# Two-layer attention-and-convolution trunk: moved squares add, head load, output-weight splits and sums

## The reference

```python
h = _rmsnorm(x, mix_norm_gain[l])
p = jnp.einsum('bsd,df->bsf', h, w_in[l])
q, k, v, conv_value, conv_gate = split(p)
q = _rope(_rmsnorm(q, q_norm_gain[l]), cos, sin)
k = _rope(_rmsnorm(k, k_norm_gain[l]), cos, sin)
attn = _dilated_attention(q, k, v)
u = conv_value * sigmoid(conv_gate)
c = silu(_layernorm(_causal_dwconv(u, conv_dw_kernel[l], conv_dw_bias[l]),
                    conv_ln_gain[l], conv_ln_bias[l]))
x = x + concat(attn, c) @ w_out[l]
h = _rmsnorm(x, ffn_norm_gain[l])
up, gate = split(causal_dwconv3(h @ w_up[l]))
x = x + (silu(gate) * up) @ w_down[l]
```

## Time and profile before

| | |
|---|---|
| median of 3 runs | 2270.85 us (2265.39, 2270.85, 2270.91) |
| profiled execution | 2272.27 us |
| its span | 2270.4 us |
| mean granted TensorE clock | 0.997 |
| TensorE busy | 2234.1 us, 98% |
| VectorE busy | 1792.8 us, 79% |
| ScalarE busy | 953.2 us, 42% |
| GpSimd busy | 131.6 us, 6% |

### The profile page before, as it was taken

The page is one execution under the profiler, slowest core; times in us unless marked ns, Lnnn a source line. Parts: engine busy times, 40 slices in busy tenths (PEclk is TensorE's granted clock), DMA queues, the critical chain, the costliest instruction groups (busy, mean ns, idle before and its releaser), DMA issues.

```text
span 2270.4 us, 31620 instructions
## 1 busy us (share of the span) xinstructions
PE 2234.1 (98%) x11128; PEld 1852.0 (82%) x11128; DVE 1792.8 (79%) x2266; ACT 953.2 (42%) x1454; POOL 131.6 (6%) x62
## 2 busy tenths in 40 slices
PE   7999999999999999999999999999999999999999
PEld 6888788888888888888888877888878888888887
DVE  5898886688777777778849998856987777777786
ACT  5322686454333333333432236755533333333331
POOL 0122001110000000000002210021000000000000
PEclk9999999999999999999999999999999999999999
DMA  4333641201111111111212245401011111111112
GB/s 155 100 88 98 177 103 29 74 19 40 54 56 55 55 55 55 55 51 42 93 38 84 84 130 158 112 11 65 19 56 56 56 50 42 55 55 55 55 40 108
DMA packets 47980, 158.25 MB, mean 70 GB/s; under 512 B 7568, under 2 KB 10256, under 8 KB 47888
## 3 DMA queue, kind: packets, MB, share of 16 engines
q1 hardware_dynamic: 47024, 154.64, 21.7%
q10 hardware_dynamic: 864, 2.36, 0.3%
HBM read 135.74 MB, written 21.23 MB: 69 GB/s over the span
## 4 chain that ended last, share of the span: by engine, by line
PE 89%; DVE 5%; DMA 2%; issue 1%; SPq 1%; ACT 1%; DVEq 0%; POOL 0%; ACTq 0%; POOLq 0%
PE mm L601 41%; PE aux L612 20%; PE mm L612 16%; PE aux L771 3%; PE aux L753 3%; PE mm L729 3%; DVE y L1617 2%; PE aux L637 1%; DMA x_hi<-qk_scratch 1%; SPq L503 1%; DVE ring L1524 1%; PE aux L699 0%; DMA x<-xT 0%; PE aux L646 0%; DMA w_raw<-weights 0%
## 5 line engine op out<-in xcount | busy, mean ns | idle before, releaser
L601 PE MATMUL mm<-x_hi,ring 128*128 128x512 f32 x1536 | 496.6, 389 | 0.0
L612 PE MATMUL aux<-hidden,ring 128*128 128x512 f32 x1920 | 439.8, 389 | 2.6 <-issue 2.1
L612 PEld LDWEIGHTS aux<-hidden,ring 128*128 128x128 f32 x1920 | 359.9, 188 | 79.5 <-issue 5.0
L612 PE MATMUL mm<-x_hi,ring 128*128 128x512 f32 x1280 | 354.4, 395 | 11.6 <-DVE x_lo L1540 11.6
L601 PE MATMUL mm<-t_all,ring 128*128 128x512 f32 x1440 | 345.9, 389 | 0.0
L601 PEld LDWEIGHTS mm<-x_hi,ring 128*128 128x128 f32 x1536 | 288.4, 188 | 59.6
L601 PEld LDWEIGHTS mm<-t_all,ring 128*128 128x128 f32 x1440 | 270.3, 188 | 56.1
L601 PE MATMUL mm<-x_lo,ring 128*128 128x512 f32 x768 | 298.8, 389 | 0.0
L612 PEld LDWEIGHTS mm<-x_hi,ring 128*128 128x128 f32 x1280 | 240.6, 190 | 62.4 <-issue 12.0
L1531 DVE TENSOR_TENSOR x<-x,aux 128x1024 f32<-128x1024 f32 x176 | 214.8, 1220 | 87.2 <-PE aux L612 86.7
L1298 ACT ACTIVATE ring<-w_raw 128x512 fp32r<-128x512 f32 x208 | 125.9, 625 | 224.1 <-PE aux L612 173.7
(11 more groups left out here) (211 smaller groups left out, 2941.5 us busy)
## 6 DMA issues: line engine op xcount, KB each, us to landing
w_raw<-weights SPq DMA_DIRECT2D x196, 512.0 KB, 3.6
qk_scratch<-m SPq DMA_DIRECT2D x64, 128.0 KB, 2.1
qk_scratch<-o SPq DMA_DIRECT2D x64, 128.0 KB, 2.1
x_hi<-qk_scratch SPq DMA_DIRECT2D x32, 256.0 KB, 6.6
ring<-qk_scratch SPq DMA_DIRECT2D x8, 512.0 KB, 4.5
ring<-qk_scratch SPq DMA_DIRECT2D x16, 256.0 KB, 6.0
k_ll_first<-qk_scratch SPq DMA_DIRECT2D x16, 256.0 KB, 6.2
x_hi<-qk_scratch SPq DMA_DIRECT2D x8, 512.0 KB, 4.7
```

Source lines behind the costliest of these rows:

```text
L601: last = pe.matmul(acc, a, b, start=start and n == 0, stop=stop and n == 2, skip_group_check=more)
L612: last = pe.matmul(acc[:, cols], a, b[:, cols], start=start and n == 0, stop=stop and n == 2)
```

## The change

- GpSimd's add of squares no longer waits for `weights_split`. In `qk_read` ScalarE makes the high part of the next weight ahead of the second square instead of behind it.
- SP issues head 1's load, with its wait on `v_unit`, ahead of the last group's 16 stores and the weight pair 24. Weight pair 26 is issued before head 5 instead of before head 3.
- The high parts of the first two output weights are made at steps 16 and 24 instead of 10 and 12, the low parts at steps 17 and 25 instead of 11 and 13.
- TensorE does three of the four pieces of `out_part(0, 1)` ahead of the mean instead of behind it.
- `norm2_sums(1)` comes one k later in its unit, and `norm2_spread(1)` too.
- In the feed-forward's first group, VectorE makes item 5's low part ahead of the two gate taps instead of behind them.

```diff
@@ SP
                 load_pair(22)
 
+                sp.wait_ge(v_unit, at(l, 2 * (V_UNITS - 1), V_UNITS + 1))
+                load_head(1, 1)
                 store_qk(QKG - 1)
                 load_pair(24)
 
-                sp.wait_ge(v_unit, at(l, 2 * (V_UNITS - 1), V_UNITS + 1))
-                load_head(1, 1)
                 plain(sp)
                 for h in range(2, HEADS):
-                    if h == 3:
+                    if h == 5:
                         load_pair(26)
@@ TensorE
+                out_part(0, 1, range(3))
                 pe.wait_ge(y_summed, at(l, CT - 1, CT - 1))
...
                 out_part(0, 0, [3])
-                out_part(0, 1, range(4))
+                out_part(0, 1, [3])
@@ TensorE
-                        if n == 0 and k == 5:
+                        if n == 0 and k == 6:
                             norm2_sums(1)
-                        if n == 1 and k == 1:
+                        if n == 1 and k == 2:
                             norm2_spread(1)
@@ ScalarE, qk_read
-                    act.activation((sa, sb_)[half][:], mm[half][:], ACT.Square).then_inc(qk_copied, 1)
                     if half:
                         hi(half, mbase + half + 2, 4, i)
+                    act.activation((sa, sb_)[half][:], mm[half][:], ACT.Square).then_inc(qk_copied, 1)
@@ ScalarE, attention
-                    if n == 10:
+                    if n == 2 * TB:
                         hi(0, U_OUT)
-                    if n == 12:
+                    if n == 3 * TB:
                         hi(1, U_OUT + 1)
@@ VectorE, attention
-                        if n == 11:
+                        if n == 2 * TB + 1:
                             lo(0, U_OUT)
-                        if n == 13:
+                        if n == 3 * TB + 1:
                             lo(1, U_OUT + 1)
@@ VectorE, group
+                    if g == 1:
+                        lo_a(1, 5)
                     gate_tap(2 * g - 1, 0, j)
                     gate_tap(2 * g - 1, 1, j)
                     move(g, 0, 0, 0, j)
                     if g == 1:
                         move(g, 0, 0, 1)
-                    lo_a(g, 5, j)
+                    else:
+                        lo_a(g, 5, j)
                     lo_a(g, 6, j)
@@ GpSimd
                     pool.wait_ge(qk_copied, at(l, 2 * QKG, 2, 2, i))
-                    pool.wait_ge(weights_split, at(l, UNITS, 8, 4, i))
                     pool.tensor_tensor(sa[:], sa[:], sb_[:], ALU.add).then_inc(qk_sqsum, 1)
```

## The result

The changed kernel takes 2277.11 us in the median of 22 runs (2272.32 to 2281.93); the kernel before takes 2269.44 in 22 runs beside them (2265.39 to 2276.09). The ratio is 1.0033, with a 95% interval of 1.0026 to 1.0041. That is 7.7 us slower, where 2.5 to 4 us faster were forecast, and it lies outside the range.

The account below looks back on a forecast made before the run. TensorE, busy 2234.1 of 2270.4 us, was taken as the bound, leaving about 36 us to gain. Terms -5.0 - 0.4 - 1.4 - 2.1 - 1.9 + 3.5 + 3.3 = -4.0 gave a median of 2266.9, range 2261.5 to 2272.5.

Parts of the forecast that it names:

- Load ahead of the stores, +3.3: Step 3's mask waits for delayed stores, 6.0 us lost, less 2.7 of waits for head 1; between +0.5 and +7.5.
- rival 4: Clock falls at four new waits, step 6's scores and output projection, 3.4 us each: slower, 2280.5 us; chance 0.08.
- Mean, +3.5: Layer norm: the later mean makes TensorE wait for GpSimd's adds before the sums, net +1.75 us in each layer.
- Add, -5.0: GpSimd's third add of squares, layer 0: without its wait it ends before TensorE asks, removing stall and low clock, 5.0 us.
- Rival 2: The slow add is a chance event the timed runs mostly lack, so the -5.0 is gone: 2271.9 us; chance 0.12.
- Output weights' parts, -1.9: Step 10: moving the high part removes TensorE's 0.94 us wait for turned probabilities, twice; no wait comes at the new steps.
- Second norm's sums, -1.4: One k later, three more matmuls (0.7 us) fill TensorE's 0.9 us wait ahead of these sums in each layer.
- Item 5, -2.1: Feed-forward: SP's load is issued about 4 us earlier, so the first `down` product's waits of 1.6 and 0.5 go.
- Second square, -0.4: High part ready 0.9 us earlier, taking 0.2 in each layer from the wait of V's fifth part on `tg`.
- port rule: VectorE and GpSimd block each other on a shared port pair; said to agree with the fourth add, not the slow third.
- queue rule: DMA engines take descriptors in ring order, so stores behind a load wait for its bytes; high end 4.2 us more, 2271.1.

Follow-up runs that it names:

- e4: Kernel before with only head 1's load and its wait put ahead of the last group's stores and weight pair 24: 2277.15 us, ratio 1.0043.
- e1: Changed kernel with head 1's load back behind the stores and weight pair 24: 2269.6 us, ratio to the kernel before 1.0008.
- e7: Kernel before with only three pieces of out_part(0, 1) put ahead of the mean: 2272.73 us, ratio 1.0020.
- e2: Changed kernel with all four pieces of out_part(0, 1) back behind the mean: 2271.84 us, ratio to the kernel before 1.0017.
- e16: e9 with the three pieces of out_part(0, 1) ahead of the mean: 2266.14 us, ratio to the kernel before 0.9991.
- e9: e3 with head 1's load behind the stores but ahead of weight pair 24: 2259.67 us, ratio to the kernel before 0.9968.
- e3: Changed kernel with both head 1's load and the mean put back: 2263.95 us, ratio to the kernel before 0.9987.
- e8: Kernel before with only item 5 ahead of the gate taps in the first feed-forward group: 2266.68 us, ratio 0.9986.
- e13: e12 with item 5 ahead of the gate taps as well: 2261.41 us, ratio to the kernel before 0.9962.
- e12: Kernel before with only head 1's load put behind the stores but ahead of weight pair 24: 2263.14 us, ratio 0.9976.
- e5: Kernel before with only GpSimd's wait on weights_split taken out, ScalarE's order unchanged: 2266.05 us, ratio 0.9997.
- e10: e3 with ScalarE's second square ahead of the high part again and output weights' parts back at steps 10 to 13: 2264.97 us, ratio 0.9991.
- e14: e9 with ScalarE's second square ahead of the high part again and output weights' parts back at steps 10 to 13: 2261.08 us, ratio 0.9969.

## Why the prediction was wrong, point by point

**Load ahead of the stores, +3.3.** The mechanism, the place and the waiting were right: mask 3 waits for the stores in both layers, TensorE's wait on it went from 2.7 to 6.5, and the wait on head 1 went. Waiting alone is up to +3.8 in e4. The step that failed is the price: a wait was priced at its own length. Measured, the move costs 5.7 to 7.5 (the changed kernel against e1) and 9.8 alone (e4). The clock falls around waits of 3.3 us, and I had put this into rival 4 at 0.08.

That rival's evidence against was the stretch from 1372 with 4 us idle at 1.00. It was one execution. Its idle time was two waits of 1.5 and 2.5 with 3.4 us of work between; the changed kernel has 3.3 in one piece, with 0.4 to 1.4 more shortly ahead. Rival 4's price of 3.4 for a fall was about right for the one at step 6 in layer 0, (0.23 + 0.11) x 10; the two others cost 1.7 each, and there were three, not four. It gave 2280.5, and the six slowest of the 22 runs read 2280 to 2282.

**Mean, +3.5.** The chain of 14.9 us decides, as worked out, and the stall splits between `out_part(1, 0)` and the sums. Waits are +1.3 in each layer rather than 1.75. The time is +4.5 by e7's ratio, +3.6 to +5.3 by the changed kernel against e2, and +5.2 to +6.5 by e16 against e9. Again the clock is missing from the term.

**Add, -5.0.** This step failed by taking an exceptional execution for the typical one. Rival 2 had it, at 0.12. Alone the add brings 0.7 in the medians, and six other profiles with the old wait have no slow add. The profiled execution was 2272.27 beside 2265.2 for executions at a clock of 1.000, and its 6.8 us of low clock were partly this add.

**Output weights' parts, -1.9.** The wait moved with them. In the new place the high part again stands ahead of a read for which TensorE waits (columns as in a timeline: start, duration, what):

```profile
281.16 1.04 ACT L990 ACTIVATE ring<-w_raw 128x1024 fp32r<-128x1024 f32 x1
282.11 0.57 ACT L1169 ACTIVATE cos<-aux 128x512 f32<-128x512 f32 x1
```

```profile
282.82 0.66 PE L771 MATMUL aux<-cos,v_third 128*64 128x128 f32 x8 [0.75 <-ACT cos L1169]
```

"In the new steps TensorE did not wait" was true of them without the 1.06 us. The step had to ask how late the read behind it may be, and did not.

**Second norm's sums, -1.4.** The wait is 1.5 in two instead of 1.8, now on `x_lo`: TensorE waits for the k-th low part ahead of the sums, and one k later that part is late. A wait that stands ahead of the moved instruction moved with it. Measured by its wait alone: -0.3. Against it stands a new wait of 0.7 in two on L601 in the first feed-forward group. It is in the waits of every profile of a kernel with this part (e3's aside) and of none without it; pair 26 has moved in the same kernels, so which of the two brings it stays open.

**Item 5, -2.1.** Right: e8 has 1.8, e13 beside e12 1.7, and the wait is gone.

**Second square, -0.4.** The wait on `tg` fell from 4.0 to 3.0, but not by the swap. In e5, e10 and e14, which have the add's change and no swap, it is 2.0 to 2.2, beside 1.4 on L1524; with the swap it is 3.0 to 3.4, beside 0.5 on L1055. The sums are nearly the same, 3.4 to 3.6 and 3.5 to 3.9. By e10 and e14 the swap is worth nothing that can be told.

**The sum.** The five other terms were to bring 5.0 + 0.4 + 1.4 + 2.1 + 1.9 = 10.8 us; with the load and the mean put back (e3) they brought 3 to 4. The load and the mean were to cost 6.8; between e3 and the changed kernel lie 10.4 to 13.2. So gains priced too high, the add above all, are the larger part of the miss, and the clock behind the new waits is the rest. By waits alone the changed kernel's list sums to about what the old one did, but the old list has the slow add's 1.6, which the other profiles lack. The forecast's sign hung on the add.

**The rules weighed.** I had said that the slow add speaks against the port rule of the Trainium skill ("SBUF — State Buffer", "SBUF: two separate sides"). The profile of e5 shows that I read it the wrong way round. VectorE, beside the add of 4.70:

```profile
108.76 0.74 DVE L1617 SCALAR_TENSOR_TENSOR y<-u_all,cpar,y 128x512 f32<-128x512 f32 x1
109.42 1.22 DVE L1524 TENSOR_TENSOR ring<-w_raw,ring 128x1024 fp32r<-128x1024 f32 x1
110.56 2.88 DVE L1617 SCALAR_TENSOR_TENSOR y<-u_all,taps_sum,y 128x512 f32<-128x512 f32 x1
```

The tap held up starts at 110.56, 2.4 after the add began, and is released near 112.9 when the add ends. The reading, inferred from these times, is that the add stood still while taps and the weight's low part ran one behind the other, then ran in about 2.3 us (the shortest adds take 2.40) while VectorE stood still. The same reading fits the 6.80 of the kernel before, 4.5 us of waiting and 2.3 of work:

```profile
164.01 0.76 DVE L1617 SCALAR_TENSOR_TENSOR y<-u_all,taps_sum,y 128x512 f32<-128x512 f32 x1
...
166.69 1.41 DVE L1524 TENSOR_TENSOR ring<-w_raw,ring 128x1024 fp32r<-128x1024 f32 x1
```

The last of the taps in a row ends at 164.77, 2.3 ahead of the add's end at 167.02, and the low part, 1.23 elsewhere, took 1.41 and had started 0.3 ahead of that end. Either engine blocks the other, as that section of the Trainium skill says. Without its old wait the add comes in the middle of the taps; why it gets its turn at once in one place and only after six of them in another, no run here shows.

The queue rule of the Trainium skill ("DMA: Bandwidth & Descriptors", "Queues, rings and completion order") agrees in part. The mask began 3.2 and 3.0 us after the last store's issue with the load ahead, and 2.0 in layer 1 before (1374.2 to 1376.23). So about 1 us can be put down to the load's bytes ahead of the stores; most of the delay is SP's own issuing, 2.8 us for the five DMAs of the load.

## What to carry to other kernels

When TensorE is busy for 98% of the time, price a new wait of 1 to 3 us by its length and by the clock that may fall around it: here a move that adds at most 3.8 us of waiting costs 5.7 to 9.8, and one that adds 2.6 costs 3.6 to 6.5. Read each run's mean clock before you trust a profile as typical, look for the same row in a second profile, and compare times at the same clock. Put a load ahead of other loads rather than ahead of stores that somebody waits for; and when an instruction is moved, ask what it now stands ahead of, and what waits stand ahead of it.

## What the runs showed of the hardware

The times in the table differ with the granted clock: from 2265.2 at 1.000 to 2276.2 at 0.995 for the same program, 2.2 us for each 0.001. TensorE's clock goes to its lower level (0.50 of 2.4 GHz, 1.2 GHz) behind waits of 0.9 to 3.3 us, in some executions and not in others. The changed kernel's stretches of 2 us around step 6's scores in layer 0, and behind the layer norm's sums, are:

```profile
254.00:256.00 2.00, 0.00 (x0) 0.00 (x0) 2.00 (x4) 0.09 (x1) 0.00 (x0) 0.87 0.00 0
256.00:258.00 2.00, 1.53 (x5) 1.24 (x6) 2.00 (x6) 1.12 (x4) 0.00 (x0) 0.50 0.03 8
...
262.00:264.00 2.00, 2.00 (x30) 1.87 (x30) 1.75 (x4) 1.24 (x2) 0.00 (x0) 0.93 0.45 100
400.00:402.00 2.00, 1.62 (x15) 1.62 (x15) 0.00 (x0) 0.00 (x0) 0.32 (x1) 1.00 0.46 174
402.00:404.00 2.00, 2.00 (x7) 1.63 (x8) 0.00 (x0) 0.18 (x1) 1.39 (x1) 0.56 0.00 0
```

In the first place the clock goes down in the wait itself and stays at 0.50 for some 6 us of full work behind it. In the second it goes down only after two waits of 0.9, nine us apart, and the sums. The fall in layer 0 around step 6 lost 3.4 us of clock at a wait of 3.3, the one behind the sums 1.7 behind waits of 0.9, and the one in layer 1 around step 6 lost 1.7 at waits of 1.4 and 3.3.

All seven waits of 3.3 us in the profiles had such a fall (two each in the changed kernel, e2 and e4, one in e8, 1.7 or 3.4 us lost each). Waits of 2.06 and 2.51 us in the kernel before, in layer 1 of the profiled execution, did not, while the same wait as the 2.06, 1.98 long in layer 0, had (0.83 from 230 to 240). What decides it in a single execution stays open; no experiment was made on it alone. e9 and e14 show that the falls can be all but removed: a mean clock of 1.000 in 12 of 14 executions, in e9 with transfers as dense as before (share 0.93).
